# Thirteen RMS norms: column sums over the channels with the squares as the loaded operand of TensorE, root and reciprocal on 128x4

## The reference, cut to what matters

```python
D_MODEL = 1024; SEQ = 512; DEPTH = 2
def rms_norm(x, w, eps=NORM_EPS):
    xf = x.astype(jnp.float32)
    y = xf * lax.rsqrt(jnp.mean(xf * xf, axis=-1, keepdims=True) + eps)
    return (y * w.astype(jnp.float32)).astype(x.dtype)
...
    for l in range(DEPTH):                        # first block: 4 norms in each of 2 layers
        h = rms_norm(x, pre_mix_w[l])
        ...
        x = x + rms_norm(y, post_mix_w[l])
        h = rms_norm(x, pre_mlp_w[l])
        y = jnp.square(jax.nn.relu(h @ w_ff1[l])) @ w_ff2[l]
        x = x + rms_norm(y, post_mlp_w[l])
...
            hn = _rms_norm(h, e_norm_mix[i])      # second block, even layer: 2 norms
            ...
            hn = _rms_norm(h, e_norm_ffn[i])
...
            hn = _rms_norm(h, o_norm_mix[i])      # odd layer: 2 norms, and the final one
            ...
            hn = _rms_norm(h, o_norm_ffn[i])
    return _rms_norm(h, final_norm)
```

## Time and profile before

| | us |
|---|---|
| median of 3 runs | 4494.3 |
| lowest, highest | 4492.37, 4518.15 |
| the profiled execution | 4491.53 |
| its span from first to last instruction | 4489.7 |

### The profile page before, as it was taken

The page is one execution under the profiler, slowest core; times in us unless marked ns, Lnnn a source line. Parts: engine busy times, 40 slices in busy tenths (PEclk is TensorE's granted clock), DMA queues, the critical chain, the costliest instruction groups (busy, mean ns, idle before and its releaser), DMA issues. The chain is left out here.

```text
span 4489.7 us, 55531 instructions
## 1 busy us (share of the span) xinstructions
PE 3978.8 (89%) x21440; PEld 3323.9 (74%) x21440; DVE 1620.2 (36%) x2849; ACT 1316.8 (29%) x2310; POOL 194.7 (4%) x160
## 2 busy tenths in 40 slices
PE   7998888998898888899797888998978879999998
PEld 5777775776677777677565776786755679999997
DVE  2365535233246443523326543333254421111112
ACT  2364533231246452323123323221223311111111
POOL 0150100000023100000000000000000000000000
PEclk9997888998998778899897989998976789999999
DMA  3100012221200001222120012222210025454443
GB/s 120 42 1 1 0 38 76 93 94 53 85 24 1 1 0 38 85 84 103 47 84 15 1 38 88 86 96 74 84 67 0 19 96 190 159 181 185 154 163 126
DMA packets 51465, 324.69 MB, mean 72 GB/s; under 512 B 6528, under 2 KB 7424, under 8 KB 20352
## 3 DMA queue, kind: packets, MB, share of 16 engines
q1 hardware_dynamic: 51328, 322.85, 20.2%
HBM read 319.68 MB, written 2.10 MB: 72 GB/s over the span
## 5 line engine op out<-in xcount | busy, mean ns | idle before, releaser
L491 PE MATMUL bank<-high 128*128 128x512 f32 x2480 | 980.8, 395 | 116.1 <-DVE low L585 81.2
L492 PE MATMUL bank<-low,high 128*128 128x512 f32 x2480 | 976.3, 394 | 0.0
L493 PE MATMUL bank<-high,low 128*128 128x512 f32 x2480 | 975.5, 393 | 0.0
L491 PEld LDWEIGHTS bank<-high 128*128 128x128 f32 x2480 | 473.0, 191 | 224.0 <-issue 67.3
L492 PEld LDWEIGHTS bank<-low,high 128*128 128x128 f32 x2480 | 473.6, 191 | 98.6
L493 PEld LDWEIGHTS bank<-high,low 128*128 128x128 f32 x2480 | 472.5, 191 | 99.9
L549 DVE TENSOR_TENSOR low<-weight_ring,high 128x2048 fp32r<-128x2048 f32 (+1 forms) x144 | 319.2, 2218 | 553.2 <-ACT high L506 553.2
L2952 PE MATMUL bank<-chosen,glu_ring 128*128 128x176 f32 x2816 | 422.0, 313 | 0.0
L2952 PEld LDWEIGHTS bank<-chosen,glu_ring 128*128 128x128 f32 x2816 | 420.1, 190 | 0.0
L506 ACT ACTIVATE high<-weight_ring 128x2048 fp32r<-128x2048 f32 (+1 forms) x144 | 266.6, 1852 | 268.9 <-PE bank L493 230.1
L2963 PE MATMUL bank<-hidden,down_ring 128*128 128x176 f32 x1408 | 211.3, 313 | 0.0
(11 more groups left out here) (489 smaller groups left out, 4847.1 us busy)
## 6 DMA issues: line engine op xcount, KB each, us to landing
glu_ring<-in_w_expert SPq DMA_DIRECT2D x88, 1024.0 KB, 4.9
weight_ring<-in_w_ff SPq DMA_DIRECT2D x64, 1024.0 KB, 4.8
down_ring<-in_w_expert_down SPq DMA_DIRECT2D x64, 704.0 KB, 5.0
weight_ring<-in_w_in SPq DMA_DIRECT2D x22, 1024.0 KB, 4.8
weight_ring<-in_w_ffe SPq DMA_DIRECT2D x22, 1024.0 KB, 4.8
weight_ring<-in_w_downe SPq DMA_DIRECT2D x16, 704.0 KB, 4.0
weight_ring<-in_w_ino SPq DMA_DIRECT2D x11, 1024.0 KB, 4.8
weight_ring<-in_w_ine SPq DMA_DIRECT2D x9, 1024.0 KB, 4.9
```

The lines of the kernel that those rows point to most:

```text
L491: nc.tensor.matmul(mem.bank[b][:, :], whole, high[:, k, :], start=(k == 0), stop=False)
L492: nc.tensor.matmul(mem.bank[b][:, :], whole, low[:, k, :], start=False, stop=False)
L493: last = nc.tensor.matmul(mem.bank[b][:, :], rest, high[:, k, :], start=False, stop=(k == kt - 1))
```

## The change: what it does

For each tile of squares, PE makes four matmuls instead of one (`token_sums`, L238 of the new kernel): a 128x128 block of squares (128 channels by 128 tokens) is the loaded operand, and one column of ones is the moving one. The result is one column of PSUM with a token on each partition; after eight tiles bank 0 holds the 512 sums as 128x4. Root (ACT) and reciprocal (DVE) then work on 128x4. To spread the factor over the partitions again, PE makes four transposes of a column that is broadcast to 128x128 (`spread_tokens`, L246) into a second PSUM bank, and DVE's multiplications read the factor from that bank instead of SBUF. The hand-over from DVE to PE (`inverted`) and from PE to DVE (`scale_ready`) are new; the wait of DVE for its own reciprocal goes. `add_norm` is changed in the same way for both of its norms.

```diff
+def token_sums(nc, mem, total, squares, k):
+
+    for t in range(TT):
+        last = nc.tensor.matmul(total[:, t:t + 1], squares[:, k, t * P:(t + 1) * P], CONST(mem.const, "ones")[:, 0:1],
+                                start=(k == 0 and t == 0), stop=(k == KD - 1 and t == TT - 1))
+    return last
+
+
+def spread_tokens(nc, mem, out, factor):
+
+    for t in range(TT):
+        last = nc.tensor.transpose(out[:, t * P:(t + 1) * P], factor[:, t:t + 1].broadcast_to([P, P]),
+                                   CONST(mem.const, "ident"))
+    return last
...
-        total = mem.bank[0]
+        total, scale = mem.bank[0], mem.bank[1]
...
             act.wait_ge(sum_ready, 1)
-            nc.scalar.activation(scale[:, :], total[:, :], ACT.Sqrt, bias=mem.eps[:, 0:1],
+            nc.scalar.activation(root[:, :], total[:, 0:TT], ACT.Sqrt, bias=mem.eps[:, 0:1],
                                  scale=1.0 / D_MODEL).then_inc(root_ready, 1)
...
             for k in range(KD):
                 pe.wait_ge(act_squares if k % 2 else dve_squares, k // 2 + 1)
-                last = nc.tensor.matmul(total[:, :], CONST(mem.const, "ones"), squares[:, k, :],
-                                        start=(k == 0), stop=(k == KD - 1))
+                last = token_sums(nc, mem, total, squares, k)
             last.then_inc(sum_ready, 1)
+            pe.wait_ge(inverted, 1)
+            spread_tokens(nc, mem, scale, root).then_inc(scale_ready, 1)
...
             primer.low(dve)
             dve.wait_ge(root_ready, 1)
-            steps.did(nc.vector.reciprocal(scale[:, :], scale[:, :]))
-            steps.settle()
+            steps.did(nc.vector.reciprocal(root[:, :], root[:, :]), inverted)
+            dve.wait_ge(scale_ready, 1)
...
-        total, x_total = mem.bank[0], mem.bank[1]
+        total, scale, x_total, x_scale = mem.bank[0:4]
...
             for k in range(KD):
                 pe.wait_ge(added_squares, k + 1)
-                last = nc.tensor.matmul(x_total[:, :], CONST(mem.const, "ones"), x_squares[:, k, :],
-                                        start=(k == 0), stop=(k == KD - 1))
+                last = token_sums(nc, mem, x_total, x_squares, k)
             last.then_inc(x_sum_ready, 1)
+            pe.wait_ge(x_inverted, 1)
+            spread_tokens(nc, mem, x_scale, x_root).then_inc(x_scale_ready, 1)
...
             dve.wait_ge(x_root_ready, 1)
-            steps.did(nc.vector.reciprocal(x_scale[:, :], x_scale[:, :]))
-            steps.settle()
+            steps.did(nc.vector.reciprocal(x_root[:, :], x_root[:, :]), x_inverted)
+            dve.wait_ge(x_scale_ready, 1)
```

More of the change, by code:

```diff
@@ L231, in low @@
                                          self.mem.w_high[:, 0, 0:n], ALU.subtract)
+def token_sums(nc, mem, total, squares, k):
[8 more added lines that the diff above has]
+    return last
 def rms_norm(nc, mem, source, gain, out, add_to=None, following=None, vectors=(), ahead=(),
              store=None):
[L241 to L245, removed]
-        total = mem.bank[0]
+    with buffers(nc, squares=[P, KD, SEQ], root=[P, TT]) as (squares, root), phase(
+            nc, "vectors_loaded", "ahead_loaded", "act_squares", "dve_squares", "sum_ready", "root_ready", "inverted",
+            "scale_ready", "made", "stored", "dve_steps", *Primer.SEMS) as (
+            block, vectors_loaded, ahead_loaded, act_squares, dve_squares, sum_ready, root_ready, inverted,
+            scale_ready, made, stored, dve_steps, *primer_sems):
+        total, scale = mem.bank[0], mem.bank[1]
         primer = Primer(nc, mem, following, primer_sems)
@@ L307, in add_norm @@
 def add_norm(nc, mem, branch, branch_gain, x, gain, out, following):
[L310 to L315, removed]
-        total, x_total = mem.bank[0], mem.bank[1]
+    with buffers(nc, squares=[P, KD, SEQ], x_squares=[P, KD, SEQ], root=[P, TT], x_root=[P, TT]) as (
+            squares, x_squares, root, x_root), phase(
+            nc, "act_squares", "dve_squares", "sum_ready", "root_ready", "inverted", "scale_ready", "normed", "added",
+            "added_squares", "x_sum_ready", "x_root_ready", "x_inverted", "x_scale_ready", "dve_steps",
+            *Primer.SEMS) as (
+            block, act_squares, dve_squares, sum_ready, root_ready, inverted, scale_ready, normed, added,
+            added_squares, x_sum_ready, x_root_ready, x_inverted, x_scale_ready, dve_steps, *primer_sems):
+        total, scale, x_total, x_scale = mem.bank[0:4]
         primer = Primer(nc, mem, following, primer_sems)
@@ L336, in _ @@
             act.wait_ge(x_sum_ready, 1)
-            nc.scalar.activation(x_scale[:, :], x_total[:, :], ACT.Sqrt, bias=mem.eps[:, 0:1],
+            nc.scalar.activation(x_root[:, :], x_total[:, 0:TT], ACT.Sqrt, bias=mem.eps[:, 0:1],
                                  scale=1.0 / D_MODEL).then_inc(x_root_ready, 1)
```

## The result

The changed kernel takes 4522.9 us (median of 20 runs, 4507.78 to 4547.9), the kernel before 4500.7 us (median of 20 runs, 4484.9 to 4518.31). The ratio is 1.0052, with a 95% interval of 1.0038 to 1.0066: 22 us or half a per cent slower, a small loss that is clear of the noise of so many runs. In the two profiled executions the span grew from 4489.7 to 4522.8 us, which is 33.1.

The account below looks back on a forecast made before the run. Norms were taken as phases between barriers, with PE's sums later than the squares and a serial tail. 63.6 - 30.7 + 0.4 = +33.3 us, less 1, on 4491.5 gave 4523.8; 2.8 more for the median made 4526, range 4490 to 4542.

Parts of the forecast that it names:

- 1 taken off: All norms: 1 us less, for norms in which the clock is still full for a moment at the start.
- The sums, +63.6: PE's one-column sums in 13 norms: 13.86 us each at half clock against 116.6 us in all, +63.6 us.
- the second rival: Norm sums: the clock falls late, full for the first 3.6 us, 10.5 us a norm; 4489 to 4515 us, chance 0.12.
- Which end of the price: Norm sums: 13.65 us at half clock or 7.3 at full clock; the prediction took 13.65.
- the first rival: Norm sums: the clock rises under them as before, 9.05 us a norm, tail 1.35 us; 4458 us, chance 0.10.
- Root, reciprocal, hand-overs, transposes, -30.7: From last sum to first multiplication: 1.86 us instead of 4.22, 2.36 less a norm, -30.7 us in all.
- Multiplications from PSUM, +0.4: DVE's 104 multiplications with the factor in PSUM: 0.747 us each instead of 0.743, +0.4 us.
- what lies behind a norm: Next phases begin at half clock as before, so nothing changes; 6 us kept in the range for clock shifts.
- The third: Norm sums: PE drains results between sums into one bank, 0.25 us a record; 4559 us, chance 0.05.

Follow-up runs that it names:

- e1_wide: The changed kernel with 128 columns of ones moved in each sum instead of one, same 64 loads a norm; 4459.1 us, ratio 0.9908 to the kernel before.
- e2_dense_first: The changed kernel with eight 512-column matmuls ahead of the sums of nine norms and of add_norm's first norm; 4564.6 us, ratio 1.0132 to the kernel before.
- e3_sums_alone: The changed kernel with one-column sums kept but root and reciprocal on 128x512 as in the kernel before; 4580.2 us, ratio 1.0190 to the kernel before.
- e6: The changed kernel with two moving columns of ones, and squares and ones rounded to fp32r; 4440.4 us, ratio 0.9846 to the kernel before.
- e5_wide_rounded: The changed kernel with 128 moving columns of ones, and squares and ones rounded to fp32r; 4451.0 us, ratio 0.9861 to the kernel before.

## Why the prediction was right

*The direction and the mechanism.* Predicted 4526, measured 4522.9; predicted against the profiled execution +32.3 us (33.3, and 1 taken off), and +33.1 in the spans. Both agreements are partly luck. Against the 4494.3 known then, 4526 is 32 us more, while the medians of 20 runs differ by 22: the kernel before turned out 6.4 us slower than its first three runs. And the spans agree because the norms gave 25.6 us, 7 less than predicted, and other phases 7.5.

*The sums, +63.6.* Measured +58.3 (174.9 - 116.6). The 13.86 us a norm are 13.6 to 13.85 in ten of the thirteen. The other three were 12.66, 12.66 and 11.84, because the clock was still full as they began: the second rival in small, 4.4 us in all where the prediction took off 1. The price was read off L991 and L997, sums with the same loads and as many records, and that is what carried the forecast.

*Which end of the price.* The step that decided was that the clock stays at 0.50 under these sums, against 7.3 us a norm at full clock. e1_wide and e2_dense_first show it as a cause and not only as a coincidence: the same loads at 128 columns let it rise and give 4459.1 us (the span is 32.8 us under that of the kernel before, where the first rival had 36), and the same one-column sums after dense work let it fall while PE never idles. The Trainium skill (TensorE: Matmul & The Clock Gate, section "Part 1: The HAM clock gate") says that the gate follows how busy PE has been of late. If that is read as the busy time of the profile, these traces don't agree: PE is busy for all of 13.7 us at 0.50 in the changed kernel. Whether the chip counts as busy something else than the profile does, no run here can tell.

*Root, reciprocal, hand-overs, transposes, -30.7.* Measured 13 x 1.72 = 22.4 us of tails against 54.7, so -32.3. Root 0.26, reciprocal 0.18 and transposes 1.11 are as predicted; the hand-over from DVE to PE is 0.06 (3642.05 to 3642.11), not 0.19. That figure was misread: each of the seven copies lasts 0.42 us and they overlap, so the first ended at 622.03 and not at 621.96, which leaves 0.12. e3_sums_alone confirms that the whole term is on the path.

*Multiplications from PSUM, +0.4.* Eight take 5.36 us instead of 5.39, -0.4 over thirteen norms: nothing is lost.

*The rest.* Sums, tails and multiplications make 58.3 - 32.3 - 0.4 = +25.6 us, and the medians differ by 22. The 7.5 us more in the two spans lie outside these three parts. Most of it lies in three phases that became 2.2 us longer each, the one behind the first norm (655.7 to 657.9) and the two behind the `add_norm` phases (375.9 and 376.0 to 378.2). The prediction had put what lies behind a norm at nothing, with 6 us of scatter; the cause of the 2.2 us stays open. (Behind `add_norm` e1 and e3 to e6, too, have 0.8 to 2.0 us more than the kernel before.) Larger changes cancel: phases shorten and lengthen with the clock. In one recurrence, 265 us behind the start of a norm's multiplications, the same work ran at full clock in the kernel before,

```profile
2240.20:2708.20 468.00, 389.22 (x2360) 0.88 0.10 33
2505.20:2525.20 20.00, 17.65 (x175) 1.00 0.00 1
3126.80:3599.00 472.20, 398.62 (x1660) 0.79 0.13 45
```

and at half clock in the changed one,

```profile
2265.90:2746.90 481.00, 403.43 (x2360) 0.85 0.09 32
2532.00:2552.00 20.00, 18.44 (x133) 0.50 0.00 1
3168.20:3627.70 459.50, 387.39 (x1660) 0.81 0.14 46
```

so that this phase was 13 us longer and the one of the last row, by the same play, 13 us shorter. Across the profiles of the experiments the first of them lies between 463 and 481 us without any change in it. I kept 6 us for such effects in the range; a single phase can move by twice that, and the 33 us between the fastest and the slowest of 20 runs of the kernel before are of the size that a few such phases give. That these stretches explain the spread of the runs is argued, not shown.

*The rivals.* The first (the clock rises) did not come for the change but was right as a price, since e1_wide is just that. The third (sums into the same bank wait for each other) did not come: a record stayed at 0.21.

## What to carry to other kernels

A reduction over the partitions on PE may put the data on either side. When only a narrow ones operand moves, check the granted clock in a window over a place that already does so, not the count of records, because here the same 64 records cost 13.8 us at one column and 9.04 at 128. Take the small layout for root and reciprocal (2.5 us a norm here) and keep the wide ones operand. Count the passes of an f32 sum before its tail: writing the squares as fp32r, where the precision allows it, took 47 us out of the norms, and the small layout with wide ones 33. And when a chain gets shorter, look at what shares its engines: three of the thirteen norms then waited for the split of the next weights.

## What the runs showed of the hardware that I had not expected

- The clock fell from 1.00 to 0.50 under one-column f32 sums with PE busy all the time, 2.3 to 4.8 us after they began behind dense work (e2_dense_first, eleven norms).
- With 128 columns, f32 sums brought the clock up after 3.3 to 6.0 us (e1_wide), and fp32r sums did not in up to 7.1 us without a gap (e5_wide_rounded).
- At half clock 512 moved columns took about 0.85 us a record in f32 and 0.43 in fp32r, while a record with a 128x128 load and 128 columns or fewer took 0.21 us in either type.
- DVE to PE through a semaphore took 0.06 us, and DVE's multiplication read its factor from PSUM as fast as from SBUF (740 and 743 ns, L315 and L298).
